# A third of the modulation as two-row products, the rest beside the projections, and residual adds on VectorE

## Chip, core, metric

The kernel runs on one core of a Trainium2 chip. The metric is the device time of one execution, in microseconds (us). A launch runs two transformer blocks after one another; the change touches the first.

## What is computed

The first block (sequence 1024, model width 1024, context 256) is, cut to what matters here:

```python
sh1, sc1, gt1, sh2, sc2, gt2 = split(silu(c) @ w_ada + b_ada, 6)        # w_ada: 1024 x 6144
csh1, csc1, ...              = split(silu(c_ctx) @ w_ada + b_ada, 6)    # only csh1, csc1 are used
hc = rmsnorm(ctx, g_pre_mix) * (1 + csc1) + csh1                        # then its k, v, gates
hx = rmsnorm(x, g_pre_mix) * (1 + sc1) + sh1                            # then @ w_in, token mixers
x  = x + gt1 * rmsnorm(yx @ w_out, g_post_mix)
hx = rmsnorm(x, g_pre_ffn) * (1 + sc2) + sh2
x  = x + gt2 * rmsnorm(conv_ffn(hx), g_post_ffn)
```

All is float32. The modulation is a product of two vectors (`silu(c)`, `silu(c_ctx)`) with a 24 MB matrix. Its rows sh1 and sc1 (with csh1, csc1) are wanted at once; gt1, sh2, sc2 and gt2 only after the token mixers.

## The kernel before

The block is a row of stages (`with Stage(...)`). Between two stages all engines meet at a barrier, so a stage begins when the last engine has left the one before. Each engine runs its own list in order; semaphores join them.

`stage_modulation` ("mod"). SP loads `w_ada` in 12 pieces of 2 MB (512 columns each) into four buffers `ada_w`; row 8p+k of the matrix is on partition p, in slot k. VectorE forms, per piece, the sum over k = 0..6 of `silu(c)[8p+k] * w[8p+k, :]` (lines 341 and 345), for the first four pieces for both condition vectors, so 16 chains of 7. ScalarE makes the eighth product (296). TensorE then sums over the partitions with a 128 x 128 matrix of ones, so that every partition holds the row, and adds the bias with a third matmul on one partition (373 to 375, `over_partitions`). ScalarE copies the rows out (302, 323). At the end VectorE multiplies five rows with the gains `graw` (359, 362) and the stage waits for `x` and `ctx`.

`stage_norm_turn` ("norm1") normalises 8 + 2 tiles with these rows and transposes them.

`stage_project_mix` ("mix") multiplies them with `w_in`. Products are split in high and low parts of type F32R: ScalarE makes the high part of the weights (208), VectorE the low one (213), TensorE runs three matmuls (219 to 221). First come 40 steps of 256 KB of weights (`w_tm`, SP line 594, two buffers; a load waits until the low part of two steps before is made, ScalarE waits until TensorE has used the step two before). A step is 12 matmuls of 512 columns, in its third group (steps 16 to 23) 6. Then come 17 blocks of 512 KB (`w_cm`, 601): 5 with a copy out by VectorE (706), then 12 with the short convolution on VectorE.

`stage_gla` works through the chunks; VectorE updates the state (950), then copies the next chunk's q and k (966, 967), on which TensorE waits (1018).

`stage_into_stream` is used as "mix_out" (8 blocks of weights, two groups of 4 token tiles) and "ffn_down" (22 blocks, two groups): split, multiply, and after each group, per tile: ScalarE sums the squares (1221), VectorE scales and roots with ScalarE (1252, 1212, 1255) and writes `y = product * inverse * gate row` (1259); GpSimd adds `y` to `x` (1234). `y` is one buffer, so the next tile's line 1259 waits for GpSimd. TensorE's next group waits tile by tile for line 1259 (`taken`), and VectorE's next split stands behind all four tiles. A third user of this function, in the second block, has no gate row; nothing of its order changes.

Of the kernel before, what the change touches and what calls it, by code (L numbers as in the profile page):

```python
# [17 lines left out]
ALU = mybir.AluOpType  # L18
ACT = mybir.ActivationFunctionType
AX = mybir.AxisListType.X  # L20
P = 128
# [3 lines left out]
D = 1024  # L25
# [202 lines left out]
def stage_modulation(core):  # L228

# [8 lines left out]
    csil = core.at("cond_silu", 108.25, [P, 2, KD])  # L238
    ones = core.at("ones", 109, [P, P])
    scaled = [core.at(f"scaled_rows{n}", kb, [P, 512]) for n, kb in enumerate((110, 202))]  # L240
    bias = core.at("ada_bias", 178, [1, 6 * D])
    SUMMED = KD - 1
    graw = core.at("gain_rows", 150, [P, 4, D])
# [3 lines left out]
    with Stage(core, "mod") as s:  # L247
        (masks_in, x_in, ctx_in, cond_in, param_in, bias_in, gain_in, silu_done, zeroed, params_turned,
         params_out, rows_done, ctx_rows_done, combined, order, sum_mm, ctx_sum, ctx_mm) = s.sems(
            "masks_in", "x_in", "ctx_in", "cond_in", "param_in", "bias_in", "gain_in", "silu_done",  # L250
            "zeroed", "params_turned", "params_out", "rows_done", "ctx_rows_done", "combined", "order",
            "sum_mm", "ctx_sum", "ctx_mm")
        scaled_done = s.sem("scaled_done")
        w_in = [s.sem(f"w_in{j}") for j in range(NW)]
        summed = [s.sem(f"summed{j}") for j in range(NW)]
        n_par = sum(len(t) for t in PARAM_ROWS)

        @s.b.gpsimd
        def _(pool):
            nc.gpsimd.memset(ones[:], 1.0).then_inc(zeroed, 1)  # L260

        @s.b.sync
        def _(sp):
# [4 lines left out]
            sp.dma_start(bias[:], dram["b_ada"]).then_inc(bias_in, 16)  # L268

            def load(i, before):  # L270
                for j in range(NW):
                    if before is not None:

                        sp.wait_ge(sum_mm, before * NW + (j + 1))
                    sp.dma_start(ada_w[:, j], dram["w_ada"][0].rearrange("(p k) n -> p k n", k=KD)
                                 [:, :, bass.ds(i * (512 * NW) + 512 * j, 512)]).then_inc(w_in[j], 16)
            run_loop(sp, 3, load)

        @s.b.scalar
        def _(act):  # L280
            act.wait_ge(cond_in, 32)
            nc.scalar.activation(csil[:], cvec[:], ACT.Silu).then_inc(silu_done, 1)
            act.dma_start(core.masks.ap().rearrange("p a b -> p (a b)"), dram["masks"]).then_inc(masks_in, 16)
# [6 lines left out]
            act.dma_start(core.ctx[:], dram["ctx"][0].rearrange("(t p) d -> p t d", p=P)).then_inc(ctx_in, 16)  # L290
            act.dma_start(core.x0[:], dram["x"][0].rearrange("(t p) d -> p t d", p=P)).then_inc(x_in, 16)
            for g, name in enumerate(("g_pre_mix", "g_post_mix", "g_pre_ffn", "g_post_ffn")):
                act.dma_start(graw[:, g, :], dram[name].to_broadcast([P, D])).then_inc(gain_in, 16)

            def scale(j, v, n):
                nc.scalar.activation(scaled[n][:], ada_w[:, j, SUMMED], ACT.Copy,
                                     scale=csil[:, v, SUMMED:SUMMED + 1]).then_inc(scaled_done, 1)

            def take(i, j):

                act.wait_ge(sum_mm, i * NW + j)
                nc.scalar.activation(flat_rows[:, bass.ds(i * (512 * NW) + 512 * (j - 1), 512)],
                                     ps[:, (j - 1) % NW, :], ACT.Copy).then_inc(rows_done, 1)

            def evacuate(i, before):
                for j in range(NW):
                    act.wait_ge(w_in[j], i * 16 + 16)
                    if before is None:
                        if j == 0:
                            act.wait_ge(silu_done, 1)  # L310
                        else:

                            act.wait_ge(sum_mm, j)
                        scale(j, 1, 0)
                        scale(j, 0, 1)
                    else:
                        act.wait_ge(sum_mm, i * NW + (j - 1 if j else 0))
                        scale(j, 0, j % 2)
                    if before is not None or j:
                        take(i, j)  # L320
                    if before is None:
                        act.wait_ge(ctx_mm, j + 1)
                        nc.scalar.activation(flat_rows[:, 6 * D + 512 * j:6 * D + 512 * j + 512],
                                             ps[:, 4 + (j + 1) % 4, :], ACT.Copy).then_inc(ctx_rows_done, 1)
            run_loop(act, 3, evacuate)
            take(3, 0)

# [2733 lines left out]
```

## Time and profile before

| | us |
|---|---|
| median of 3 runs (3810.71 to 3820.34) | 3814.72 |
| the profiled execution, its own time | 3825.96 |
| its span in the trace | 3824.1 |
| mod, up to norm1's first instruction | 120.8 |
| norm1 | 44.0 |
| mix, the 40 steps | 107.9 |
| mix_out with its entry and exit | 125.9 |

A view of the trace is one execution. "Granted clock" is the mean TensorE clock of a stretch: 1.00 is 2.4 GHz, 0.50 is 1.2 GHz. A row of the timeline merges neighbours of one kind (x2, x8) and shows in brackets how long the engine sat idle before and what ended that.

### The profile page before, as it was taken

Reading aid. Unit: us, or ns where it says so; the run is one execution under the profiler, and the core shown is the slowest. Engines: PE = TensorE matmul, PEld = TensorE weight load, DVE = VectorE, ACT = ScalarE, POOL = GpSimd, SP = SyncE. Lnnn points to the kernel's source line nnn. Section 1 sums busy time; section 2 is a strip of 40 time slices with the busy share of each in tenths; the row PEclk is TensorE's granted clock in tenths of the full one; section 3 lists DMA queues with packets and bytes.
Section 4 is the critical chain, followed back from the end, with each engine's and each line's share of the span. In section 5 each row is a group of like instructions: output and inputs, shape, how many; then the busy total and the mean of one; then the engine's idle time right before and its main releaser. Section 6 shows DMA issues by size and latency. Waiting matters only on the chain. (4 is left out here: it accounts for less than half of the span.)

```text
span 3824.1 us, 58374 instructions
## 1 busy us (share of the span) xinstructions
PE 3169.6 (83%) x24565; PEld 2477.3 (65%) x24565; DVE 2125.8 (56%) x2592; ACT 1340.5 (35%) x1776; POOL 381.6 (10%) x249
## 2 busy tenths in 40 slices
PE   6699956679999899587987878858799872999995
PEld 1378845568888678473666574747566662888884
DVE  6632254356666533427366665767211347988885
ACT  1320143322111232327333333434200222777774
POOL 0200011210000000302011111111000000122120
PEclk7699967879999999799998888969899976999997
DMA  8131102211111323200201010010310334999996
GB/s 323 57 101 40 38 1 95 82 44 50 49 44 51 108 88 102 79 18 28 68 2 66 1 43 24 4 47 18 102 50 22 127 139 154 377 395 396 399 394 214
DMA packets 219997, 424.22 MB, mean 111 GB/s; under 512 B 13120, under 2 KB 122642, under 8 KB 219538
## 3 DMA queue, kind: packets, MB, share of 16 engines
q1 hardware_dynamic: 212434, 394.75, 29.0%
q0 software_dynamic: 4608, 16.78, 1.7%
q10 hardware_dynamic: 2753, 9.66, 0.6%
q8 instruction: 167, 2.74, 0.3%
q14 instruction: 35, 0.29, 0.0%
HBM read 387.61 MB, written 33.55 MB: 110 GB/s over the span
## 5 line engine op out<-in xcount | busy, mean ns | idle before, releaser
L213 DVE TENSOR_TENSOR w_exp_low<-w_exp,w_exp_high 128x2048 fp32r<-128x2048 f32 x192 | 437.7, 2290 | 54.2 <-ACT w_exp_high L208 54.2
L208 ACT ACTIVATE w_exp_high<-w_exp 128x2048 fp32r<-128x2048 f32 x192 | 368.0, 1920 | 123.2 <-PE psum L221 123.2
L219 PE MATMUL psum<-ffn_high,w_high 128*128 128x512 f32 x704 | 275.0, 391 | 9.2 <-DVE w_low L213 9.2
L220 PE MATMUL psum<-ffn_low,w_high 128*128 128x512 f32 x704 | 274.8, 390 | 0.0
L221 PE MATMUL psum<-ffn_high,w_low 128*128 128x512 f32 x704 | 274.8, 390 | 0.0
L1375 DVE SCALAR_TENSOR_TENSOR ffn_hidden<-u_padded,param_columns,ffn_hidden 128x1024 f32 (+1 forms) x176 | 226.2, 1285 | 23.8 <-DVE ffn_hidden L1371 0.2
L219 PE MATMUL psum<-w_exp_high,x_turned_high 128*128 128x512 f32 x512 | 202.9, 396 | 7.0 <-DVE w_exp_low L213 7.0
L221 PE MATMUL psum<-w_exp_high,x_turned_low 128*128 128x512 f32 x512 | 200.0, 391 | 0.0
L220 PE MATMUL psum<-w_exp_low,x_turned_high 128*128 128x512 f32 x512 | 199.8, 390 | 0.0
L2301 DVE COPY inverse<-psum 64x512 f32<-64x512 f32 x192 | 121.8, 637 | 75.5 <-PE psum L2136 50.4
L219 PE MATMUL psum<-ffn_down_w_split,ffn_down_lhs_split 128*128 128x512 f32 x352 | 140.6, 400 | 23.3 <-DVE ffn_down_lhs_split L213 17.4
L219 PEld LDWEIGHTS psum<-ffn_high,w_high 128*128 128x128 f32 x704 | 132.8, 189 | 37.3 <-DVE w_low L213 9.6
L2235 ACT ACTIVATE inverse<-psum 64x512 f32<-64x512 f32 x192 | 107.0, 557 | 130.3 <-PE psum L2136 105.2
L220 PEld LDWEIGHTS psum<-ffn_low,w_high 128*128 128x128 f32 x704 | 132.7, 189 | 27.7
L221 PEld LDWEIGHTS psum<-ffn_high,w_low 128*128 128x128 f32 x704 | 132.7, 189 | 27.6
L2573 DVE TENSOR_TENSOR gates_sb<-gates_sb,psum 128x1024 f32<-128x1024 f32 x16 | 19.5, 1221 | 232.3 <-PE psum L2521 232.3
L513 PE MATMUL psum<-masks,norm_h 128*128 128x128 f32 x272 | 60.4, 397 | 102.1 <-POOL norm_h L502 63.9
L213 DVE TENSOR_TENSOR ffn_down_w_split<-ffn_down_ring,ffn_down_w_split 128x1024 fp32r<-128x1024 f32 x44 | 53.9, 1225 | 158.7 <-ACT ffn_down_lhs_split L208 158.7
L220 PE MATMUL psum<-ffn_down_w_split,ffn_down_lhs_split 128*128 128x512 f32 x352 | 139.6, 397 | 0.0
L221 PE MATMUL psum<-ffn_down_w_split,ffn_down_lhs_split 128*128 128x512 f32 x352 | 139.3, 396 | 0.0
L1350 ACT ACTIVATE ffn_hidden<-ffn_hidden (+1 forms) x22 | 23.3, 1061 | 295.4 <-DVE ffn_hidden L1375 295.4
L219 PE MATMUL psum<-mix_out_w_split,mix_out_lhs_split 128*128 128x512 f32 x256 | 102.8, 402 | 27.7 <-DVE mix_out_lhs_split L213 20.9
(431 smaller groups left out, 7867.4 us busy)
## 6 DMA issues: line engine op xcount, KB each, us to landing
w_exp<-in_exp_w_gate SPq DMA_DIRECT2D x32, 2048.0 KB, 11.1
w_exp<-in_exp_w_up SPq DMA_DIRECT2D x32, 2048.0 KB, 10.4
w_exp<-in_exp_w_down SPq DMA_DIRECT2D x32, 2048.0 KB, 11.2
ada_weights<-in_w_ada SPq DMA_DIRECT2D x12, 2048.0 KB, 14.0
w_raw<-in_w_up SPq DMA_DIRECT2D x44, 512.0 KB, 3.8
ffn_down_ring<-in_w_down SPq DMA_DIRECT2D x44, 512.0 KB, 3.6
mix_out_ring<-in_w_out SPq DMA_DIRECT2D x32, 512.0 KB, 3.7
mixers_hT<-hidden SPq DMA_DIRECT2D x4, 4096.0 KB, 13.0
```

Of the source, the lines that this page charges most:

```text
L208: return nc.scalar.activation(out, src, ACT.Copy, scale=scale)
L213: return nc.vector.tensor_tensor(out, src, high.bitcast(F32), ALU.subtract)
L219: nc.tensor.matmul(out, left[0], right[0], start=start, stop=False)
L220: nc.tensor.matmul(out, left[0], right[1], start=False, stop=False)
L221: return nc.tensor.matmul(out, left[1], right[0], start=False, stop=stop)
L513: ins = nc.tensor.transpose(ps[:, 2 * (t % 4) + k // 4, (k % 4) * P:(k % 4 + 1) * P], hbuf[:, t % SLOTS, k * P:(k + 1) * P], core.mask(M_ID))
L1350: nc.scalar.activation(block(i * 2 + (j - 1)), block(i * 2 + (j - 1)), ACT.Silu).then_inc(silu_done, 1)
L1375: ins = nc.vector.scalar_tensor_tensor(out=out, in0=src, scalar=weight, in1=out, op0=ALU.mult, op1=ALU.add)
L2235: nc.scalar.activation(place[rows[1], :], ps[rows[1], inverse_bank(n, 1), columns], ACT.Copy).then_inc(inv_lower[n % 2], 1)
L2301: nc.vector.tensor_copy(place[rows[0], :], ps[rows[0], inverse_bank(n, 0), columns]).then_inc(inv_upper[n % 2], 1)
L2573: nc.vector.tensor_tensor(sg[:, h], sg[:, h], ps[:, 4 * h + 2:4 * h + 4, :], ALU.mult).then_inc(parts, 1)
```

## The change

- Mod computes only the first 4 of the 12 pieces. TensorE multiplies them directly: the stationary operand is `csil[:, k, :]`, 128 rows by 2 columns (both conditions), the moving one a slot of `ada_w`; 8 matmuls of 512 columns per piece give a pair of rows in PSUM. VectorE adds the bias (`pairs`, 2 x 512). A second matmul per row, with a 2 x 128 selector, spreads it to all partitions; ScalarE copies the shifts out, VectorE the gain rows with `(1 + scale) * g`. `x` and `ctx` are loaded by SP behind the four pieces.
- The other 8 pieces (rows of `c` alone) move into mix: SP loads them in 16 halves of 1 MB into two buffers, VectorE adds slot after slot into `mod_rows`, 64 instructions put by the list `room` behind its work of each step, and TensorE sums over the partitions with one matmul of ones after each of blocks 5 to 12; ScalarE copies out. The bias goes into partition 0 by DMA after GpSimd has zeroed the rows.
- The three later gain rows are loaded and multiplied in gla, by VectorE, before its loop.
- In `stage_into_stream` the add moves from GpSimd to VectorE, with four `y` buffers: in the middle of a product one add behind each of the next splits, at the end interleaved.

```diff
@@ stage_modulation, TensorE
+            def spread_rows(j):
+                pe.wait_ge(pair_done, j + 1)
+                if j >= 2:
+                    pe.wait_ge(shifts_done, 2 * j - 2)
+                for v in range(2):
+                    nc.tensor.matmul(ps[:, spread_bank(j, v), :], select[:, v, :], pairs[:, j], start=True, stop=True
+                                     ).then_inc(spread, 1)
+            pe.wait_ge(silu_done, 1)
+            pe.wait_ge(selects, 2)
+            for j in range(NW):
+                pe.wait_ge(w_in[j], 16)
+                for k in range(KD):
+                    ins = nc.tensor.matmul(ps[0:2, j, :], csil[:, k, :], ada_w[:, j, k], start=(k == 0),
+                                           stop=(k == KD - 1))
+                ins.then_inc(pair_mm, 1)
+                if j:
+                    spread_rows(j - 1)
...
+            spread_rows(NW - 1)
@@ stage_project_mix
+    room = [0] * 5 + [2] * 3 + [1] * 5 + [2] * 3 + [0] * (KD + 2) + [1] * 3 + [2] * (3 + KD) + [4] * (irregular + 1)
+    step_of = [at for at, n in enumerate(room) for _ in range(n)][:4 * HALVES]
+    last_step = [step_of[4 * h + 3] for h in range(HALVES)]
+    ada_loads = {0: [0, 1]}
+    for h in range(2, HALVES):
+        ada_loads.setdefault(last_step[h - 2] + (3 if last_step[h - 2] + 3 < NQ else 4), []).append(h)
@@ TensorE
+                if n in sums_at:
+                    m = n - irregular
+                    first = ADA + 512 * m
+                    pe.wait_ge(ada_used, 2 * m + 2)
+                    if m >= 2:
+                        pe.wait_ge(ada_out, m - 1)
+                    nc.tensor.matmul(ps[:, 6 + m % 2, :], core.ones[:], flat_rows[:, first:first + 512], start=True,
+                                     stop=True).then_inc(ada_sum, 1)
@@ VectorE
+            def modulate(step):
+                for m in [m for m, at in enumerate(step_of) if at == step]:
...
+                    if k == 0:
+                        dve.wait_ge(ada_in[h % 2], 16 * (h // 2 + 1))
...
+                    ins = nc.vector.scalar_tensor_tensor(out=acc, in0=ada_w[:, h % 2, k], scalar=core.csil[:, n, 0:1],
+                                                         in1=acc, op0=ALU.mult, op1=ALU.add).then_inc(ada_order, 1)
@@ stage_gla, VectorE
+            dve.wait_ge(gain_in, 48)
+            nc.vector.tensor_tensor(rows[:, R_GP1], rows[:, R_GP1], graw[:, 0], ALU.mult)
+            nc.vector.scalar_tensor_tensor(out=rows[:, R_G2], in0=rows[:, R_G2], scalar=1.0, in1=graw[:, 1],
+                                           op0=ALU.add, op1=ALU.mult)
+            nc.vector.tensor_tensor(rows[:, R_GP2], rows[:, R_GP2], graw[:, 2], ALU.mult)
@@ stage_into_stream
-        if gate_row is not None:
-            @s.b.gpsimd
-            def _(pool):
-                pool.wait_ge(x_in, 16)
-                for t in range(TT):
-                    pool.wait_ge(taken, t + 1)
-                    nc.gpsimd.tensor_tensor(x[:, t], x[:, t], y[:], ALU.add).then_inc(added, 1)
+            def add(t):
+                dve.wait_ge(x_in, 16)
+                dve.wait_ge(taken, t + 1)
+                nc.vector.tensor_tensor(x[:, t], x[:, t], y[t % G][:], ALU.add).then_inc(added, 1)
```

VectorE's list in mix, around the step in which the fifth half (the second use of buffer 0 after its reload) begins; the change alone. `mix_tm_high` is the high part of a step's weights, `mix_ada_in0` the landing of a half in buffer 0, `mix_ada_order` the instruction before:

```order
L213 TENSOR_TENSOR w_tm_split<-w_tm,w_tm_split 128x512 [waits mix_tm_high]
L690 SCALAR_TENSOR_TENSOR mod_rows<-ada_weights_late,cond_silu,mod_rows 128x512 [waits mix_ada_order] x2
L213 TENSOR_TENSOR w_tm_split<-w_tm,w_tm_split 128x512 [waits mix_tm_high]
L690 SCALAR_TENSOR_TENSOR mod_rows<-ada_weights_late,cond_silu,mod_rows 128x512 [waits mix_ada_order]
L690 SCALAR_TENSOR_TENSOR mod_rows<-ada_weights_late,cond_silu,mod_rows 128x512 [waits mix_ada_order,mix_ada_in0]
L213 TENSOR_TENSOR w_tm_split<-w_tm,w_tm_split 128x512 [waits mix_tm_high] x2
```

Before, the same place held only the rows of line 213. The low part of step 16 now stands behind an instruction that waits for the load of half 4, which SP issues with step 16's own weights.

VectorE's list in mix_out where the second group begins; the change alone (waits left out, since semaphores are numbered anew there). The numbers behind `mix_out_y` are the four buffers:

```order
L1289 SCALAR_TENSOR_TENSOR mix_out_y_3800<-psum,mix_out_stat,mod_rows 128x1024
L213 TENSOR_TENSOR mix_out_w_split<-mix_out_ring,mix_out_w_split 128x1024
L213 TENSOR_TENSOR mix_out_lhs_split<-gla_out_cm,mix_out_lhs_split 128x512
L1267 TENSOR_TENSOR x_stream<-x_stream,mix_out_y_3797 128x1024
L213 TENSOR_TENSOR mix_out_w_split<-mix_out_ring,mix_out_w_split 128x1024
L213 TENSOR_TENSOR mix_out_lhs_split<-gla_out_cm,mix_out_lhs_split 128x512
L1267 TENSOR_TENSOR x_stream<-x_stream,mix_out_y_3798 128x1024
```

Before, the list was the same without line 1267, which GpSimd ran in its own list.

## Rows read from the trace of the kernel before

**Rows 1.** The page, its part 1: busy time of TensorE and GpSimd.

```profile
PE 3169.6 (83%) x24565; PEld 2477.3 (65%) x24565; DVE 2125.8 (56%) x2592; ACT 1340.5 (35%) x1776; POOL 381.6 (10%) x249
```

**Rows 2.** Windows: mod, mix's 40 steps, its later blocks, mix_out; then DMA's rate.

```profile
core 0: us, PE busy (x) PEld busy (x) DVE busy (x) ACT busy (x) POOL busy (x), PEclk, DMA share, GB/s
0.00:120.80 120.80, 74.84 (x99) 22.74 (x99) 85.51 (x120) 21.14 (x34) 0.41 (x5) 0.74 0.76 280
164.80:272.70 107.90, 100.16 (x425) 80.63 (x426) 33.62 (x50) 28.51 (x45) 0.00 (x0) 0.96 0.36 99
345.00:480.00 135.00, 130.84 (x576) 108.03 (x576) 35.95 (x31) 15.55 (x15) 1.76 (x4) 0.99 0.16 40
15.00:30.00 15.00, 5.44 (x9) 2.07 (x10) 10.06 (x15) 1.93 (x3) 0.00 (x0) 1.00 1.03 402
```

**Rows 3.** Mod: VectorE's group of line 345, its wait for the weights, norm1's first instruction.

```profile
L345 DVE SCALAR_TENSOR_TENSOR mod_rows<-ada_weights,cond_silu,mod_rows 128x512 f32<-128x512 f32 (+1 forms) x96 | 72.2, 752 | 3.4
DVE mod_rows L341 <- DMA ada_weights<-in_w_ada: 27.5, 7, 15.8
120.83 1.28 ACT L431 ACT_TABLE_LOAD   x1 [6.59 <-PEq L185]
```

**Rows 4.** DMA issues: KB each, median us from issue to landing.

```profile
ada_weights<-in_w_ada SPq DMA_DIRECT2D x12, 2048.0 KB, 14.0
w_tm<-in_w_in SPq DMA_DIRECT2D x40, 256.0 KB, 2.6
alibi<-in_alibi SPq DMA_DIRECT2D x1, 1536.0 KB, 6.0
```

**Rows 5.** Timeline: weight loads of float32 matmuls of 512 columns in a row.

```profile
483.90 0.33 PEld L780 LDWEIGHTS psum<-gate_low,w_gates 32*128 32x128 f32 x1 [0.52 <-issue]
484.76 0.33 PEld L780 LDWEIGHTS psum<-gate_low,w_gates 32*128 32x128 f32 x1 [0.52 <-issue]
```

**Rows 6.** Windows (columns as in rows 2): stretches with TensorE busy, and what followed.

```profile
41.00:44.40 3.40, 3.40 (x4) 0.99 (x4) 0.00 (x0) 0.52 (x1) 0.00 (x0) 0.50 1.04 399
44.40:47.80 3.40, 1.25 (x3) 0.29 (x2) 3.23 (x5) 1.81 (x3) 0.00 (x0) 0.99 1.05 386
170.90:174.20 3.30, 3.30 (x9) 2.53 (x9) 0.00 (x0) 0.00 (x0) 0.00 (x0) 0.50 0.42 148
174.20:177.60 3.40, 3.40 (x17) 2.78 (x16) 0.69 (x1) 0.63 (x1) 0.00 (x0) 1.00 0.09 11
481.20:494.30 13.10, 13.10 (x18) 5.79 (x18) 6.01 (x4) 7.84 (x7) 0.00 (x0) 0.50 0.00 0
```

**Rows 7.** Timeline of mix: VectorE at step 16, ScalarE at step 18.

```profile
213.64 0.69 DVE L213 TENSOR_TENSOR w_tm_split<-w_tm,w_tm_split 128x512 fp32r<-128x512 f32 x1 [2.03 <-ACT w_tm_split L208]
217.07 0.63 ACT L208 ACTIVATE w_tm_split<-w_tm 128x512 fp32r<-128x512 f32 x1 [0.74 <-DMA w_tm<-in_w_in]
```

**Rows 8.** Timeline: gain products at mod's end; gla's first wait of TensorE for VectorE.

```profile
114.58 3.48 DVE L359 SCALAR_TENSOR_TENSOR mod_rows<-mod_rows,gain_rows 128x1024 f32<-128x1024 f32 x3
117.98 2.35 DVE L362 TENSOR_TENSOR mod_rows<-mod_rows,gain_rows 128x1024 f32<-128x1024 f32 x2
532.55 2.08 PE L1018 MATMUL psum<-q_chunk,k_chunk 64*128 64x128 f32 x16 [2.04 <-DVE k_chunk L967]
```

**Rows 9.** Timeline of mix_out (first six rows) and ffn_down (last): scales and adds.

```profile
684.70 1.28 DVE L1259 SCALAR_TENSOR_TENSOR mix_out_y<-psum,mix_out_stat,mod_rows 128x1024 f32<-128x1024 f32 x1
686.31 0.17 DVE L1255 RECIPROCAL mix_out_stat<-mix_out_stat 128x1 f32<-128x1 f32 x1 [0.27 <-ACT mix_out_stat L1212]
688.63 1.28 DVE L1259 SCALAR_TENSOR_TENSOR mix_out_y<-psum,mix_out_stat,mod_rows 128x1024 f32<-128x1024 f32 x1 [2.15 <-POOL x_stream L1234]
698.66 2.86 DVE L213 TENSOR_TENSOR mix_out_lhs_split<-gla_out_cm,mix_out_lhs_split 128x512 fp32r<-128x512 f32 x1
738.70 1.28 DVE L1259 SCALAR_TENSOR_TENSOR mix_out_y<-psum,mix_out_stat,mod_rows 128x1024 f32<-128x1024 f32 x1
751.48 2.34 POOL L1234 TENSOR_TENSOR x_stream<-x_stream,mix_out_y 128x1024 f32<-128x1024 f32 x1 [1.47 <-DVE mix_out_y L1259]
1434.04 2.86 DVE L213 TENSOR_TENSOR ffn_down_lhs_split<-ffn_hidden,ffn_down_lhs_split 128x512 fp32r<-128x512 f32 x1
```

More of the change, by code:

```diff
@@ L299, in take @@
[L299 to L324, printed above, removed]
@@ L348, in _, with gains @@
-            run_loop(dve, 3, sums)
+            dve.wait_ge(masks_in, 16)
+            for v in range(2):
+                nc.vector.tensor_copy(select[:, v, :], core.masks[0:2, M_ID, v:v + 1].to_broadcast([2, P])
+                                      ).then_inc(selects, 1)
+            dve.wait_ge(bias_in, 16)
+            def gains(j):
+                for v in range(2):
+                    dve.wait_ge(spread, 2 * j + v + 1)
+                    first = 512 * (j - 2)
+                    nc.vector.scalar_tensor_tensor(out=place(j, v), in0=ps[:, spread_bank(j, v), :], scalar=1.0,
+                                                   in1=graw[:, first:first + 512], op0=ALU.add, op1=ALU.mult
+                                                   ).then_inc(gains_done, 1)
@@ L350, in _ @@
+            for j in range(NW):
+                dve.wait_ge(pair_mm, j + 1)
+                nc.vector.tensor_tensor(pairs[:, j], ps[0:2, j, :], bias[:, 512 * j:512 * j + 512], ALU.add
+                                        ).then_inc(pair_done, 1)
+            dve.wait_ge(gain_in, 16)
+            gains(2)
+            gains(3)
             dve.wait_ge(params_turned, 1)
@@ L553, in stage_project_mix @@
     scx = core.at("sc_part", 40, [P, T])
+    flat_rows = core.rows.ap().rearrange("p a d -> p (a d)")
+    ada_w = core.at("ada_weights_late", 170, [P, 2, KD // 2, 512])
+    ADA, HALVES = 2 * D, 2 * (4 * D // 512)
     def tokens(k, t0, n):
@@ L1242, in split, with out @@
                 low_part(nc, l_split[:, q % 2, 1], lhs(k, g), l_split[:, q % 2, 0]).then_inc(low, 1)
-            def out(g):
+            def add(t):
+                dve.wait_ge(x_in, 16)
+                dve.wait_ge(taken, t + 1)
+                nc.vector.tensor_tensor(x[:, t], x[:, t], y[t % G][:], ALU.add).then_inc(added, 1)
+            def out(g, k):
+                if k:
+                    if gate_row is not None:
+                        add(g * G + k - 1)
+                    return
                 for t in range(g * G, g * G + G):
@@ L1256, in out @@
                     dve.wait_ge(order, 2 * t + 2)
-                    if t:
-                        dve.wait_ge(added, t)
-                    nc.vector.scalar_tensor_tensor(out=y[:], in0=product(t), scalar=stat[:, 0, t:t + 1], in1=gate_row,
-                                                   op0=ALU.mult, op1=ALU.mult).then_inc(taken, 1)
+                    if t >= G:
+                        dve.wait_ge(added, t - G + 1)
+                    nc.vector.scalar_tensor_tensor(out=y[t % G][:], in0=product(t), scalar=stat[:, 0, t:t + 1],
+                                                   in1=gate_row, op0=ALU.mult, op1=ALU.mult).then_inc(taken, 1)
+                    if k is None and t > g * G:
+                        add(t - 1)
+                if k is None and gate_row is not None:
+                    add(g * G + G - 1)
             with_splits(split, out)
```

182 lines of the change are left out of this document (89 added, 93 removed).

## The prediction

> **What bounds the kernel now.** I read the page first: TensorE is busy 83% of the span, GpSimd 10% [rows 1]. Then the windows of the stages that the change touches. In mod TensorE is busy 74.84 of 120.80 us, VectorE 85.51, DMA moves 280 GB/s [rows 2]: no engine is full, and a chain bounds the stage. Its longest member is VectorE's sums: line 345 alone takes 72.2 us, 96 times 752 ns, and VectorE waits 27.5 us more for weights, 15.8 of them for the first piece [rows 3]. Mod ends when norm1's table load starts, at 120.83. In mix TensorE bounds: busy 100.16 of 107.90 us in the 40 steps (VectorE 33.62) and 130.84 of 135.00 in the later blocks [rows 2]. VectorE has room there, TensorE has none, so whatever goes on TensorE in mix is paid in full. In mix_out and ffn_down the waits around the end of a group are the place: the scale of a tile waits 2.15 us for GpSimd's add of the one before [rows 9].
>
> **Mod.** Removed: all 16 chains and their matmuls. New is a chain of SP, TensorE and a short end.
>
> The first piece. Before, it was there at 15.8 us, beside masks, parameters and a part of `ctx` on the other queue. Now masks, one gain row and parameters stand beside it, and `x` and `ctx` come later: I take 14.0, with 12 and 15.8 as ends. Further pieces of 2 MB at 402 GB/s [rows 2] come every 5.2 us, and all the rest (6.3 MB of weights, 5.2 MB of `x` and `ctx`) is in by 14.0 + 11.5/0.402 = 43 us.
>
> TensorE. A float32 matmul call leaves two records. At 1.2 GHz, records of 512 columns start 0.86 us apart (483.90, 484.76) [rows 5]; at 2.4 GHz half of it, 0.43. The products are 4 pieces x 8 slots x 2 = 64 records, the spreads 8 x 2 = 16. At 1.2 GHz a piece takes 13.7 us, at 2.4 GHz 6.9: either is more than the 5.2 us of a load, so from the first piece on TensorE is the bound and does not stop. Which clock is the large question. The nearest rows: float32 matmuls of 128 rows by 512 columns kept the engine busy from 41.0 to 44.4 at a granted 0.50, and it was 0.99 after that; the F32R matmuls of mix did the same at 174.2, 4.5 us after their start. Against it: line 780, with 32 of 128 rows [rows 5], was busy 13.10 of 13.10 us and stayed at 0.50 [rows 6]. The new products fill all 128 rows but 2 of 128 columns, and no row here shows that shape. I take the rise, because the data streamed through the engine, 128 rows of 512 float32, is that of the first of these rows. With 5.1 us at 1.2 GHz (6 records), 58 x 0.43 = 24.9 us for the other products, 16 x 0.43 = 6.9 for spreads, some 2 us for changes between the two shapes and 0.5 for the transposes, TensorE ends at 14.0 + 5.1 + 24.9 + 6.9 + 2.5 = 53.4. VectorE's last gain row (0.75, like line 345) and parameter copies (0.6) lie behind it, less what overlaps; barrier 0.5. Norm1 starts at 54.8 instead of 120.8: **-66.0**. `x` at 43 is hidden, with 10 us to spare.
>
> **Mix, the 40 steps.** The 64 accumulations of 0.75 us lie beside TensorE. A step is 2.72 us; VectorE has 0.61 (low part), at times 0.6 (copy out), and at most 2 x 0.78: 2.2 of 2.72. Cost nothing while TensorE has 12 matmuls a step; if that cover is gone (steps 16 to 23, half as long), `room` has zeros. The loads are another matter. 1 MB: between 2.6 us for 256 KB and 6.0 for 1536 KB [rows 4] I estimate 4.7, with the step's weights in front 5.4. In steps 31 to 39 a half is issued 5.4 us before its use and TensorE's own slack is 1.4 more: nothing. The half used at step 15 is the exception (the first order listing): it is issued with step 16's weights, 3.5 us before VectorE arrives, so VectorE waits 2 us; the low part of step 16, at 213.64 before [rows 7], slips by 1.5, and steps 16 to 23 are paced by loads (ScalarE waits for DMA at 217.07 [rows 7]) that are issued behind low parts, so it is not caught up: +1.5. The weights behind each 1 MB land up to 0.7 us later, in a slack of 1.3 before ScalarE; for step 19 perhaps 0.5. **+2.0**, with 0 and 8 as ends (8 if the halves of steps 31 to 39 each stall 1 us more). GpSimd's zeroing of 4096 elements and SP's wait for it end before step 2's load is due.
>
> **Mix, the blocks.** TensorE is full there [rows 2], so 8 sums of ones cost 8 x 2 x 0.43 = **+6.9**; with a start-up each up to 9. ScalarE's 8 copies and VectorE's waits for the last halves (each half is issued behind the low part of a block of 10.9 to 13.8 us) are hidden; a half later than 6.5 us would hold the copy of the next block: 0 to 2.
>
> **Gla.** Three gain products, at 1.16 each as in mod [rows 8], stand between the second state update and the q and k copies on which TensorE waits (532.55, idle 2.04) [rows 8]: **+3.5**. The three loads of 512 KB are issued 9 us earlier, hidden; ends 0 and 5.
>
> **Mix_out and ffn_down.** In the middle, scales came 3.85 us apart: 684.70, 688.63, and so on to 696.33. Without the wait a tile takes what leads from one scale to the next reciprocal, 684.70 to 686.31, and 0.2: 1.81. Three tiles save 6.1. The split behind them took 2.86 instead of 0.68 while GpSimd added [rows 9]: another 2.2. The next product starts 8.2 us earlier, the same in ffn_down, where the split at 1434.04 shows the same 2.86 [rows 9]: -16.6 with its slightly longer first wait. The adds (1.16 each) follow a split of 1.8 within a step of 5.4: hidden. At the end of each: scales from 738.70, then per tile scale 1.2, add 1.15, statistics and root 0.6; the last add ends at 749.9 instead of 751.48 + 2.34 = 753.8 [rows 9]. Less 0.4 for stores closer together: -3.5 each. **-23.6** in all; ends -28 and -14.
>
> **Sum.** -66.0 + 2.0 + 6.9 + 3.5 - 23.6 = **-77.2**. Against the profiled execution's own 3825.96 that is 3748.8; that execution stands 11.2 us above the median of the runs, so for the median 3814.72 - 77.2 = **3737.5**.
>
> **Rivals.**
> (B) The clock stays at 1.2 GHz in mod. For it speaks line 780 [rows 6]; against it the stretches of 128 rows. Then 80 records x 0.86 + 3 = 71.8 us follow 14.0, mod ends at 87.2 with its tail, and 32 of the 66 are gone: 3814.7 - 45 = **3770**. [...]
> (C) Slower than before: the loads in mix hold VectorE, and with it the low parts. It decides from the point where 1 MB takes over 7.2 us (5.4 and the slack of 1.8). The row for it is mod's own 14.0 [rows 4], of twice the size and beside another queue: 13 halves x 6.8 = 88, and 9 times a step's high and low part laid bare, 12: 3737 + 100 = **3837**. Against it: 256 KB in 2.6 us and DMA at 99 GB/s in these steps [rows 2]; the new loads bring it to some 200 of 402.
> (D) The moved adds return what they save: if each of the first three adds held a split, 2 x 3 x 1.2, and the end gained nothing: 3737 + 14 = **3752**; inside the range.
> (E) Mod waits for `x` instead of TensorE. It would have to land after 54, so all loads run below 290 GB/s from 14.0 on, against the 402 [rows 2] of before; at mod's own mean of 280 [rows 2] it costs 1 us and leaves the sum as it is.
>
> **Chances.** My forecast with its variants (D, E) 0.70, B 0.25, C 0.02; 0.03 for something that returns nearly all. A change under 0.3% (11.4 us) can't be told from none here. Faster 0.96, same 0.02, slower 0.02. The likeliest case's own range is 3728 to 3748; the range given has to reach B: 3728 to 3774.
>
> **What would show it.** In the profile after: norm1's table load near 55 (B: near 87); the granted clock over mod's products 1.00 after the first 3 to 7 us (B: 0.50), and product records 0.43 apart; a wait of VectorE for `ada_weights_late` of about 2 us once and none over 1 us in steps 31 to 39 (C: many of 5 and more); TensorE's line 628 with 16 records of 0.6; in gla TensorE's first wait for `k_chunk` 5.5 instead of 2.04; four scales 1.8 apart. Wrong in the main thing if mod ends where B says.

## The result, and the profile after

| us | before | changed |
|---|---|---|
| median of the runs | 3814.69 (3810.71 to 3820.34, 4 runs) | 3746.51 (3742.48 to 3755.25, 4 runs) |
| ratio | | 0.9823, 95% interval 0.9801 to 0.9845 |
| the same pair in a later comparison | 3823.80 (9 runs) | 3752.93 (5 runs), ratio 0.9819, 0.9803 to 0.9834 |
| profiled execution, its span | 3825.96, 3824.1 | 3742.48, 3740.7 |

The forecast was 3737.5 in a range of 3728 to 3774; 68 to 71 us came where 77 were expected. Between the two profiled executions it is 83.5 us, where the forecast had 3748.8 for the second and 3742.48 came. The time by stage tells more. Each stage starts with a table load of ScalarE (ACT_TABLE_LOAD, 1.28 us), and the difference of two of them is a stage's length. Two profiles of each kernel stand side by side; the second ones are runs 9 and 12 below.

| stage, us | before | before, 2nd | changed | changed, 2nd | forecast of the change |
|---|---|---|---|---|---|
| mod | 120.83 | 117.46 | 54.80 | 54.79 | -66.0 |
| norm1, gla_out, norm2 | 107.1 | 107.1 | 107.4 | 107.4 | 0 |
| mix | 312.70 | 310.00 | 325.01 | 324.56 | +8.9 |
| gates and gla | 127.59 | 127.83 | 130.48 | 130.69 | +3.5 |
| mix_out | 125.64 | 127.14 | 112.68 | 113.08 | -11.8 |
| ffn_up | 497.23 | 497.64 | 496.11 | 496.29 | 0 |
| ffn_down | 279.03 | 279.20 | 264.51 | 264.52 | -11.8 |
| up to norm3 | 1570.1 | 1566.3 | 1491.0 | 1491.3 | |
| the second block, whose code is the same | 2254.0 | 2255.6 | 2249.7 | 2261.9 | 0 |

**Mod.** The page's part 1, which answers to [rows 1]:

```profile
PE 3129.3 (84%) x24565; PEld 2456.4 (66%) x24565; DVE 2108.9 (56%) x2568; ACT 1327.3 (35%) x1756; POOL 344.6 (9%) x234
```

Windows of mod (columns as in [rows 2]):

```profile
0.00:54.80 54.80, 38.36 (x83) 8.40 (x83) 6.34 (x13) 3.89 (x7) 0.41 (x5) 0.99 0.76 282
...
14.00:19.90 5.90, 4.98 (x6) 0.76 (x7) 0.00 (x0) 0.00 (x0) 0.00 (x0) 1.00 1.02 365
19.90:31.20 11.30, 11.30 (x27) 2.13 (x25) 0.68 (x1) 0.00 (x0) 0.00 (x0) 1.00 1.05 393
```

And the timeline of TensorE there, with norm1's first instruction, which stood at 120.83 in [rows 3]:

```profile
14.92 16.38 PE L338 MATMUL psum<-ada_weights,cond_silu 128*2 128x512 f32 x32 [14.92 <-DMA ada_weights<-in_w_ada]
31.23 1.98 PE L331 MATMUL psum<-row_pairs,select_row 2*128 2x512 f32 x4
33.14 7.03 PE L338 MATMUL psum<-ada_weights,cond_silu 128*2 128x512 f32 x16
...
51.30 1.98 PE L331 MATMUL psum<-row_pairs,select_row 2*128 2x512 f32 x4
...
54.80 1.28 ACT L381 ACT_TABLE_LOAD   x1 [12.08 <-PEq L185]
```

VectorE's 85.5 us are gone and TensorE works without a stop from the first piece on. The sum's units are in the traces: a float32 matmul call left two records (line 338: 64 for 32 calls; line 780 of before: 24 for 12), and records of 512 columns started 0.86 us apart at a granted 0.50 [rows 5, 6] and 0.43 apart at 1.00 (19.90:31.20 above). The profile prints the granted clock only as a share; 1.2 and 2.4 GHz are the forecast's names for 0.50 and 1.00, and nothing is worked out from them. Six records took the first 5 us (0.81 to 0.86 us apart), the other 26 of the first 32 are 0.43 apart (the second window counts the sixth once more): the clock rose as forecast, after 6 records. The window prints a clock of 1.00 for both stretches, but the trace's first entry of the clock stands at 19.96 us; before it the spacing of records is the better witness.

**Mix.** Its waits of VectorE and TensorE (line waited for, total, times, longest), and three rows of its timeline:

```profile
DVE mod_rows L690 <- DMA ada_weights_late<-in_w_ada: 28.4, 9, 6.3
PE psum L219 <- DVE w_tm_split L213: 13.6, 6, 6.9
PE psum L219 <- ACT out_gate L638: 3.2, 1, 3.2
PE psum L219 <- DVE qT L721: 2.2, 1, 2.2
```

```profile
110.94 0.63 ACT L208 ACTIVATE w_tm_split<-w_tm 128x512 fp32r<-128x512 f32 x1 [7.97 <-DMA w_tm<-in_w_in]
...
144.43 0.45 SPq L562 DMA_DIRECT2D ada_weights_late<-in_w_ada  x1
...
151.26 0.75 DVE L690 SCALAR_TENSOR_TENSOR mod_rows<-ada_weights_late,cond_silu,mod_rows 128x512 f32<-128x512 f32 x1 [3.85 <-DMA ada_weights_late<-in_w_ada]
```

The places can be read off the low parts (VectorE L213), 57 in both kernels, each counted from its own mix's start. The low part of step 2 is 2.08 us later than before and that of steps 4 to 15 is 1.15; step 16 is 4.30 later, steps 19 to 39 some 5.2. (Seven profiles have this mix: here, runs 1, 3, 5, 6, 7 and 9. Step 39 is 4.1 to 5.5 later in them.) In the blocks each sum of ones then adds 0.905:

```profile
308.23 1.22 DVE L213 TENSOR_TENSOR w_cm_split<-w_cm,w_cm_split 128x1024 fp32r<-128x1024 f32 x1 [9.11 <-ACT w_cm_split L208]
...
320.01 1.23 DVE L213 TENSOR_TENSOR w_cm_split<-w_cm,w_cm_split 128x1024 fp32r<-128x1024 f32 x1 [5.97 <-ACT w_cm_split L208]
```

The group of the sums on TensorE (busy, mean ns of one, idle before):

```profile
L628 PE MATMUL psum<-mod_rows,ones 128*128 128x512 f32 x16 | 8.2, 590 | 0.0
```

It is 11.78 us from one block's low part to the next, 10.88 before; eight sums are 7.2. Between, after step 41, TensorE waits 3.2 us for `out_gate` in every profile (3.5 in run 11). In the first profile of before the granted clock was at 0.50 for 6.8 us around the end of that wait, in its second not at all, in the changed kernel for 3.4: so mix of before was 312.7 and 310.0, and the changed one is 12.3 or 15.0 longer, by which profile of before one takes. Run 2, whose mix is that of before, has 312.8.

**Gla** lost what was forecast. TensorE's first wait for `k_chunk` was 2.04 in [rows 8]:

```profile
478.16 1.23 DVE L1006 TENSOR_TENSOR mod_rows<-mod_rows,gain_rows_late 128x1024 f32<-128x1024 f32 x1
479.31 1.21 DVE L1007 SCALAR_TENSOR_TENSOR mod_rows<-mod_rows,gain_rows_late 128x1024 f32<-128x1024 f32 x1
480.44 1.21 DVE L1009 TENSOR_TENSOR mod_rows<-mod_rows,gain_rows_late 128x1024 f32<-128x1024 f32 x1
...
482.52 2.08 PE L1046 MATMUL psum<-q_chunk,k_chunk 64*128 64x128 f32 x16 [5.45 <-DVE k_chunk L990]
```

**Mix_out and ffn_down.** The scales of mix_out, the split and the first add, then the end, which answer to [rows 9]:

```profile
633.20 1.28 DVE L1289 SCALAR_TENSOR_TENSOR mix_out_y<-psum,mix_out_stat,mod_rows 128x1024 f32<-128x1024 f32 x1
...
635.01 1.28 DVE L1289 SCALAR_TENSOR_TENSOR mix_out_y<-psum,mix_out_stat,mod_rows 128x1024 f32<-128x1024 f32 x1
...
641.05 0.68 DVE L213 TENSOR_TENSOR mix_out_lhs_split<-gla_out_cm,mix_out_lhs_split 128x512 fp32r<-128x512 f32 x1
641.65 1.22 DVE L1267 TENSOR_TENSOR x_stream<-x_stream,mix_out_y 128x1024 f32<-128x1024 f32 x1
...
678.92 1.28 DVE L1289 SCALAR_TENSOR_TENSOR mix_out_y<-psum,mix_out_stat,mod_rows 128x1024 f32<-128x1024 f32 x1
...
687.82 2.35 DVE L1267 TENSOR_TENSOR x_stream<-x_stream,mix_out_y 128x1024 f32<-128x1024 f32 x2
```

The scales are 1.81 apart, as forecast. From the first scale to the split's end it is 8.5 us instead of 16.8 (684.70 to 701.52), from the first scale of the end to the end of the last add 11.25 instead of 15.1. From the first scale of the middle to the first scale of the end ffn_down gained 10.3 us where mix_out gained 8.3, for another reason: the clock. The same 3.6 us behind the split, before and then changed:

```profile
1437.00:1440.60 3.60, 3.60 (x9) 2.83 (x10) 1.83 (x2) 0.65 (x2) 0.00 (x0) 0.51 0.67 156
```

```profile
1363.20:1366.80 3.60, 3.60 (x16) 2.96 (x17) 3.12 (x4) 1.53 (x2) 0.00 (x0) 1.00 0.46 146
```

Nine products instead of sixteen. Before, TensorE waited 6.9 us in all for these scales and the split (longest 2.6), its products stood 0.43 apart instead of 0.23 from 1429.20 on, and the granted clock was still 0.50 to 0.51 here; in the changed kernel none of these waits is over 0.2 us and the clock is 1.00. At half the speed these 3.6 us cost 1.8.

### The profile page after: what moved, and what is told of

The parts are those of the page before. It is cut to its first block and busy times, and to the rows that moved or that the text cites. A ratio compares the mean times of both kernels' runs of the same rounds, so it can differ in the third digit from the quotient of the medians.

```text
span 3740.7 us, 58197 instructions
## 1 busy us (share of the span) xinstructions
PE 3129.3 (84%) x24565; PEld 2456.4 (66%) x24565; DVE 2108.9 (56%) x2568; ACT 1327.3 (35%) x1756; POOL 344.6 (9%) x234
## 5 line engine op out<-in xcount | busy, mean ns | idle before, releaser
L213 DVE TENSOR_TENSOR w_exp_low<-w_exp,w_exp_high 128x2048 fp32r<-128x2048 f32 x192 | 437.7, 2290 | 54.2 <-ACT w_exp_high L208 54.2
L221 PEld LDWEIGHTS psum<-ffn_high,w_low 128*128 128x128 f32 x704 | 132.6, 188 | 27.5
L213 DVE TENSOR_TENSOR ffn_down_w_split<-ffn_down_ring,ffn_down_w_split 128x1024 fp32r<-128x1024 f32 x44 | 53.9, 1225 | 152.0 <-ACT ffn_down_lhs_split L208 152.0
L1909 PE MATMUL psum<-mixers_hT,w_rkv 128*128 128x512 f32 x288 | 124.9, 593 | 0.0
```

The lines of the kernel that those rows point to most:

```text
L213: return nc.vector.tensor_tensor(out, src, high.bitcast(F32), ALU.subtract)
L221: return nc.tensor.matmul(out, left[1], right[0], start=False, stop=stop)
L1909: ins = nc.tensor.matmul(ps[:, 2 * NEXT[n] + h, :], w[n][:, kt], hT[:, kt, 512 * h:512 * h + 512], start=(kt == 0), stop=(kt == KD - 1))
```

## Experiments

The untouched second block took 2250 to 2266 us over all profiles. The touched stages repeat more closely. Where their code is the changed kernel's, ffn_down took 263.5 to 264.6 us, mix_out 112.5 to 113.7, mod 53.35 to 55.16 (its first piece came at 13.9 to 15.4) and mix 324.2 to 325.1, in two profiles 327.0 and 327.3 (see run 8). Where it is that of before, mod took 117.5 to 121.3 and mix 310.0 to 312.8. So sizes below are read from stages, each good to about such a spread, and the medians only where they tell kernels apart. Times of before run on the same chip stand with each group.

### Runs 1 to 3: the residual adds

Beside a before of 3818.50 (3809.93 to 3825.03). Run 1 puts `stage_into_stream` back as it was:

```diff
+    y = core.at(f"{name}_y", scratch_kb + 4, [P, D])
...
+            @s.b.gpsimd
...
+                    nc.gpsimd.tensor_tensor(x[:, t], x[:, t], y[:], ALU.add).then_inc(added, 1)
...
-                      (132, 136, 140, 144))
```

> The changed kernel with stage_into_stream as it was before: one buffer y, the add on GpSimd. The theory of the prediction (mix_out and ffn_down give 23.6 us, and in the two profiles they gave 13.0 + 14.5 = 27.5): this run takes 24 to 28 us more than the changed kernel, 3770 to 3775, 41 to 45 below the kernel before. Rival: the untouched stages drifted by some 5 us between the two profiles, and a part of the 27.5 is such drift; then it lies 15 to 20 us above the changed kernel.

Measured: 3777.41 (3774.20 to 3778.80), ratio 0.9890 against 0.9823 and 0.9819 of the changed kernel: 26 us above it. Mix_out 126.7, ffn_down 278.0: +14.0 and +13.5. The theory holds; what differed between profiles lies elsewhere.

Run 2 is the kernel before with only the new `stage_into_stream`.

> The kernel before with only the new stage_into_stream. If the parts of the change are independent, 24 to 28 us below the kernel before (3787 to 3791), with mix_out some 12 to 13 and ffn_down some 12 to 14.5 shorter in the profile and everything else unchanged. Rival: the parts share something (another start of the transfers, another clock), and this one and the one with the stream undone do not add up to the whole, by more than 5 us.

Measured: 3792.97 (3786.99 to 3803.88), ratio 0.9931 (0.9918 to 0.9945), 25.5 us below before. Mix_out 113.7, ffn_down 264.3: -12.0 and -14.8. Run 1 lies 41.1 below before and this one 25.5: 66.6 together, against 68 to 71 for the whole, within the 5 us that the rival asked for. The parts are independent as far as that tells.

Run 3 keeps the four buffers and gives the adds back to GpSimd:

```diff
-                nc.vector.tensor_tensor(x[:, t], x[:, t], y[t % G][:], ALU.add).then_inc(added, 1)
...
+                    nc.gpsimd.tensor_tensor(x[:, t], x[:, t], y[t % G][:], ALU.add).then_inc(added, 1)
```

> The changed kernel with four buffers y but the adds on GpSimd, as before. It tells the buffer from the engine. By the prediction's split of the middle (6.1 us from the wait, 2.2 from the stretched split behind it): the scales come 1.8 apart, but GpSimd still adds (2.35 each, four in a row behind the scales), VectorE's splits beside it are stretched to some 2.9, once or more often, and at the end of each stage the last add ends some 4 us after the last scale: 3 to 10 us slower than the changed kernel, 3749 to 3757. Rival: the buffer is everything and the engine nothing: the same as the changed kernel within 2 us. Second rival: GpSimd slows every VectorE operation beside it, the scales too, and half of the gain is lost (12 us or more).

Measured: 3763.24 (3760.96 to 3767.07), ratio 0.9853. Mix_out 118.2, ffn_down 270.0: each 5.5 above the changed kernel and 8.0 to 8.5 below run 1. Of the 27.5 us the buffers give 16.5 and the engine 11.0, which is more than my 3 to 10. The size is near the second rival's 12, its mechanism did not come: the scales still take 1.28 and stand 1.81 apart. Timeline behind the first group of mix_out, and TensorE's clock after it:

```profile
634.53 10.39 POOL L1262 TENSOR_TENSOR x_stream<-x_stream,mix_out_y 128x1024 f32<-128x1024 f32 x4 [64.39 <-DVE mix_out_y L1290]
...
638.54 1.28 DVE L1290 SCALAR_TENSOR_TENSOR mix_out_y<-psum,mix_out_stat,mod_rows 128x1024 f32<-128x1024 f32 x1
639.81 2.92 DVE L213 TENSOR_TENSOR mix_out_w_split<-mix_out_ring,mix_out_w_split 128x1024 fp32r<-128x1024 f32 x1
...
642.65 2.82 DVE L213 TENSOR_TENSOR mix_out_lhs_split<-gla_out_cm,mix_out_lhs_split 128x512 fp32r<-128x512 f32 x1
...
645.52 0.80 PE L219 MATMUL psum<-mix_out_w_split,mix_out_lhs_split 128*128 128x512 f32 x1 [3.98 <-DVE mix_out_lhs_split L213]
```

```profile
645.60:651.60 6.00, 6.00 (x14) 4.71 (x15) 1.61 (x2) 0.00 (x0) 0.00 (x0) 0.50 0.62 178
```

Both splits beside the queued adds are stretched (2.92 and 2.82 instead of 1.22 and 0.68: +3.8 us), and TensorE, which waited 4.0 us for them, runs its next 6 us at a granted 0.50 (14 products where 26 would go: some 2.7 us). Less 0.8 that this kernel gains at the end and 0.4 at its start, that is about the 5.5. At the end the buffers alone do the work: from the first scale of the end to the next stage it is 18.2 us before, 14.5 in the changed kernel and 13.7 here, so there the move to VectorE costs 0.8. The scale beside the same adds keeps its 1.28. The splits read both inputs from SBUF, the scale one of them from PSUM; whether this is the cause, no run shows.

### Run 4: where the late loads stand in mix

```diff
-    room = [0] * 5 + [2] * 3 + [1] * 5 + [2] * 3 + [0] * (KD + 2) + [1] * 3 + [2] * (3 + KD) + [4] * (irregular + 1)
+    room = [0] * 5 + [2] * 3 + [1] * 5 + [2] * 2 + [1] + [0] * (KD + 3) + [2] * (5 + KD) + [4] * (irregular + 1)
...
-    ada_loads = {0: [0, 1]}
+    ada_loads = {2: [0], 3: [1], KD * 3: [4], KD * 3 + 1: [5]}
...
```

> The changed kernel with the late modulation halves loaded elsewhere: halves 0 and 1 behind the weights of steps 2 and 3 and not in front of step 2's, half 4 and 5 with steps 24 and 25 and not with 16 and 18, and no sum of half 4 in step 15. In the profiles mix's 40 steps lost 1.15 us at step 2 (its weights behind 2 MB) and 4.0 at steps 15 to 19. Theory: both come from the place of these loads in SP's queue, and go: low part of step 39 is 0 to 0.5 us later than before instead of 5.2, the kernel 4 to 5.5 us faster than the changed one. Rival: the loss at steps 16 to 19 is DMA shared among all (short steps paced by loads that only got slower) and comes back wherever the 1 MB lands: then 1 to 2 us at most.

Measured in the profile: mix 321.3 instead of 325.0 (324.2 to 325.1 in the five profiles without the fall of the clock of run 8). The low part of step 2 is 0.5 us earlier than before, that of step 23 0.6 earlier; then steps 24 to 28, where halves 4 and 5 now land, lose 1.6, and step 39 is 1.0 later than before, where the changed kernel is 5.2 later. So 4.2 of the 5.2 us (3.0 to 4.5, against each of the seven profiles) hung on the place of these loads in SP's queue, and the rival has the rest: 1 MB landing between short loads cost something at the new place too. The median, 3751.12 (3747.32 to 3754.68), ratio 0.9822 (0.9809 to 0.9835), can't be told from the changed kernel's: 4 us drown in the second block, which took 2265.6 us in this profile, the longest of all.

### Runs 5 and 6: TensorE's clock in mod

Each with a single execution, beside a before of 3821.86. Run 5 takes 32 of the 128 rows, and so leaves out three quarters of each sum:

```diff
-                    ins = nc.tensor.matmul(ps[0:2, j, :], csil[:, k, :], ada_w[:, j, k], start=(k == 0),
+                    ins = nc.tensor.matmul(ps[0:2, j, :], csil[0:32, k, :], ada_w[0:32, j, k], start=(k == 0),
```

> The changed kernel with the products of mod over 32 of the 128 rows of each slot (so the modulation sums a quarter of its terms); 2 output columns as before, and all loads unchanged. Record spacing in mod: 0.85 us at 1.2 GHz, 0.43 at 2.4. My reason for the high clock was the 128 rows of data streamed through the engine, as against line 780 of before with 32 rows: then the products stay 0.85 apart throughout and mod ends near 87 us instead of 54.8. Rival: the rows do not decide, an engine that is kept busy without a gap rises either way: then mod ends at 54.8 as in the changed kernel, and line 780 stayed low for another reason.

```profile
15.35 27.46 PE L338 MATMUL psum<-ada_weights,cond_silu 32*2 32x512 f32 x32 [15.35 <-DMA ada_weights<-in_w_ada]
...
46.45 13.81 PE L338 MATMUL psum<-ada_weights,cond_silu 32*2 32x512 f32 x16
```

32 records in 27.46 us, 16 in 13.81: 0.86 each, from the first to the last, without a gap in 66 us. The spreads, which are the same in both kernels, stand 0.85 to 1.0 us apart here and 0.43 to 0.54 in the changed kernel, so it is the clock and not the shape of the product; the trace's first entry of the clock is only at 140.3 us. Mod ends at 87.3, rival B's 87.2. With the same loads and as many products the clock rose after 5 us for 128 rows and not for 32, as in line 780 [rows 6]: the ground on which the forecast chose between its two prices is shown.

Run 6 issues piece j only behind piece j-1's products, so that TensorE waits:

```diff
+                if j:
+                    sp.wait_ge(pair_mm, j)
                 sp.dma_start(ada_w[:, j], dram["w_ada"][0].rearrange("(p k) n -> p k n", k=KD)
```

> The changed kernel with each piece of 2 MB in mod issued only when the products of the piece before are done, so that TensorE waits some 7 us (2 MB at 390 to 400 GB/s and the start) before each of the pieces 1 to 3. [...] Worst case: 4 pieces x 13.7 + 3 x 7 + 15 + 4 = 95 us for mod. Theory that a wait of this length costs the clock for as long as the first start did (6 records): each piece 6.9 + 2.5 = 9.4, mod ends near 15 + 4 x 9.4 + 3 x 7 + 4 = 78. Rival, the clock survives a wait of 7 us: mod ends near 54.8 + 21 - 6 = 70.

```profile
14.56 9.52 PE L340 MATMUL psum<-ada_weights,cond_silu 128*2 128x512 f32 x16 [14.56 <-DMA ada_weights<-in_w_ada]
32.73 8.97 PE L340 MATMUL psum<-ada_weights,cond_silu 128*2 128x512 f32 x16 [8.65 <-DMA ada_weights<-in_w_ada]
...
50.24 8.75 PE L340 MATMUL psum<-ada_weights,cond_silu 128*2 128x512 f32 x16 [6.63 <-DMA ada_weights<-in_w_ada]
...
68.44 9.89 PE L340 MATMUL psum<-ada_weights,cond_silu 128*2 128x512 f32 x16 [7.54 <-DMA ada_weights<-in_w_ada]
```

After each wait (6.6 to 8.7 us) the first 4 to 7 records are 0.85 apart, at a granted 0.50, and the rest 0.43, at 0.99 to 1.00: a piece takes 8.8 to 9.9 us instead of 7.03. The worst case, every record 0.85 apart, did not come, and the clock did not survive the wait either. Mod ends at 85.45, more than my 78, because 8.5 to 9.5 us passed from one piece's end to the next start instead of 7, and 7.1 us from the last piece's end to norm1 instead of 4 (the last spreads were 0.85 apart again). In the changed kernel, whose pieces are queued at once, TensorE's only wait for a piece is the first, of 14.92 us, and its products are 0.43 apart from the seventh record on.

### Runs 7 and 8: an earlier start, and sums where TensorE waits

Also one execution each. Run 7 loads every piece as two halves with a wait each:

```diff
+                for a in range(2):
+                    sp.dma_start(ada_w[:, j, 4 * a:4 * a + 4], dram["w_ada"][0].rearrange("(p k) n -> p k n", k=KD)
+                                 [:, 4 * a:4 * a + 4, 512 * j:512 * j + 512]).then_inc(w_in[2 * j + a], 16)
```

> The changed kernel with each 2 MB piece of mod loaded as two transfers of 1 MB (slots 0 to 3, 4 to 7), each with its own wait. TensorE is the bound of mod from the first piece on (72 of its records in one stretch), so an earlier start should move the whole stage: first product near 10 instead of 14.92, mod ends 4 to 5.5 us earlier (49 to 51 instead of 54.8). Rival: the stage is then bound by the loads (x and ctx in at 43, weights at 29) or the two halves land together, and less than 2 us come of it.

First product at 9.79, mod 50.13 instead of 54.80: -4.7 (-3.2 to -5.0 against the six profiles with whole pieces). TensorE was the bound of the whole stage, and `x`, which the sum called hidden with 10 us to spare, still was.

Run 8 moves the sums of ones and the gain products:

```diff
 stage_gates, tensor, behind u == 3
+            for m in range(8):
+                nc.tensor.matmul(ps[:, late_bank[m], :], core.ones[:], late(m), start=True, stop=True
+                                 ).then_inc(ada_sum, 1)
...
 stage_gla, vector, first step, behind qk_staged
+                        nc.vector.tensor_tensor(rows[:, R_GP1], rows[:, R_GP1], graw[:, 0], ALU.mult)
...
```

> The changed kernel with the eight sums of ones moved out of mix's blocks, where TensorE is full, to the end of TensorE's work in gates, where it waits 23 us for gla (ScalarE copies them out in its own waits of 2.0 and 6.1 us there), and the three gain products of gla moved from in front of the q and k copies into VectorE's waits within the first step. Theory: mix gets 7.2 us shorter (8 x 0.905; 325.0 to 317.8), gates and gla together 3.4 us (130.5 to 127.1), 10 to 11 in all. Rival: ScalarE's copies in gates push its exponentials (its waits there are for VectorE, so a copy that comes late holds the chain): gates gets 1 to 4 us longer and half of it is given back.

Measured: mix 319.7 (-5.3), gates and gla 127.7 (-2.8). The eight steps of 11.78 are 10.88 again, so the 7.2 are there. But 1.9 came back, 1.6 of it at one place, TensorE's wait for the `qT` copy at the start of block 5: there VectorE was held by the late halves (four waits of 5.4 to 6.5 us there), the wait is 1.4 us in before, 2.2 in the changed kernel and 2.5 here, and behind it the clock fell in this run:

```profile
284.40:287.80 3.40, 3.40 (x9) 2.64 (x8) 0.96 (x2) 0.00 (x0) 0.00 (x0) 0.50 0.81 222
```

That fall does not belong to this edit. It stands at the same place in runs 5 and 6, whose mix is the changed kernel's and took 327.3 and 327.0 us, and in none of the other five profiles of that mix. Nor does the length of the wait decide alone: the fall came behind waits of 2.3 and 3.5 us there and not behind one of 2.6 in run 1. The rival on ScalarE in gates did not come.

### Runs 9 to 11: the changed kernel again, and all mended

Beside a before of 3823.80 (3813.02 to 3827.49). Run 9 is the changed kernel; run 10 the edits of runs 4, 7 and 8 together.

> The changed kernel itself, unchanged, beside the next two on the same chip. The untouched stages (the second block) varied by 10 us between the profiles so far, the touched ones by 0.3, so the stage sums (-66.0, +12.3, +2.9, -13.0, -14.5: -78 us) should come again within 1 us, while the median lies 66 to 82 us under that of the kernel before. Rival: the median difference of the first comparison, 68.2 us, is the true one, because the new kernel loses some 10 us in untouched stages each time: then their sum in this profile is again above that of before.

> The changed kernel with the three mendings that were measured apart: half pieces in mod (-4.7), late loads moved in mix (-4.2 in the 40 steps), sums of ones in gates and gain products in gla's waits (mix -7.2 without the clock's dip, gates and gla -2.8). Additive: 18 to 20 us below the changed kernel of this call in the touched stages, about 3728 if that is 3747. Rival: a part is given back by the clock (each new wait of TensorE in mix's blocks of 2.6 us or more can start a stretch of 3.4 us at 1.2 GHz, 1.7 us each): 14 to 17.

Run 9: 3752.93 (3750.09 to 3759.27), the stages within 0.5 us of the first profile (table). Run 10: 3733.62 (3724.95 to 3735.57), ratio 0.9759 (0.9742 to 0.9776), 19.3 us below run 9 and 90 below before. Mod 49.50 (-5.3), mix 314.8 (-9.8), gates and gla 127.8 (-2.9): 18.0 in stages. The rival is in it too: the fall of the clock at block 5 came in this run as in run 8 (and as in runs 5 and 6, without these edits).

Run 11 adds a warm-up before the first piece:

```diff
+            pe.wait_ge(ones_done, 1)
+            for n in range(24):
+                nc.tensor.matmul(ps[:, 3, 0:P], ones[:], ones[:], start=True, stop=True)
```

> The kernel of e10 with 24 products of 128 x 128 ones (discarded) on TensorE from 1 us on, before the first piece of mod is there at 9.8. If what the clock needs is a busy engine, it is high when the first products start: all records 0.43 apart, mod 2.6 us shorter (6 records x 0.43). Rival: the small products (128 columns) do not raise it, or the engine is still in them when the piece lands: mod the same or up to 2 us longer.

```profile
1.00 8.51 PE L336 MATMUL psum<-ones 128*128 128x128 f32 x48 [1.00 <-POOL ones L263]
9.44 3.60 PE L343 MATMUL psum<-ada_weights,cond_silu 128*2 128x512 f32 x8
14.19 3.60 PE L343 MATMUL psum<-ada_weights,cond_silu 128*2 128x512 f32 x8 [1.16 <-DMA ada_weights<-in_w_ada]
```

The discarded products go from 0.21 to 0.11 apart after 6 us, and the real ones are 0.43 apart from the first. But of the 2.6 us at most a part arrives: mod is 48.77, 0.7 less than in run 10 and 1.4 less than in run 7, whose mod is the same as run 10's. The engine now waits 1.16 us for the second half, at 14.19, and 0.46 for the next piece, at 18.25. The bound has moved to the loads. 3732.23 (3728.25 to 3738.63), the same as run 10.

### Run 12: the kernel before again

> The kernel before, unchanged, for a second profile of it. Open is why the medians differ by 68 to 71 us where the touched stages differ by 79: if the time behind norm3's start is taken as median less 1.8 less the end of ffn_down in the profile, it is 2243 to 2252 us for the kernel before and 2254 to 2263 for all with the new mod. First reading: the first profile of before (3825.96) was a slow one and its untouched part is normally some 8 us shorter: then this profile is near 3815, with norm3 starting at 1570.1 within 0.5 and the rest 2243 to 2250. Second reading: the rest is 2254 here too, with the same span near 3824, and profiles of this kernel are slower than its other executions. Third: norm3 starts earlier than 1570, so that the stages of the first block vary in this kernel.

Measured: 3820.54 (3813.42 to 3823.81, 11 runs), span 3821.9, norm3 at 1566.3, the rest 2255.6. The third reading holds in part: mod was 3.4 us shorter (VectorE waited 24.4 us for weights, 27.5 in [rows 3]) and mix 2.7 (no fall of the clock after step 41), while mix_out was 1.5 longer for a fall of its own. Run 2, whose mod and mix are those of before, has 121.3 and 312.8, as the first profile. So the first block gained some 75 to 79 us by the profiles and 68 to 71 by the medians. The remaining 4 to 11 us lie in the second block, whose code is the same and which varied by 16 us between profiles. It took 2254.0 to 2256.8 us in the three profiles with the old mod and 2249.7 to 2265.6, 2259.4 in the mean, in the eleven with the new one. Whether it is a little longer behind the new first block, or this is chance, stays open.

## Why the prediction was right

**Mod: right, in size and reason.** The sum gave norm1 at 54.8; it was 54.80. The first piece came at 14.92 instead of 14.0 and TensorE ended a little earlier than 53.4 in return. The choice of the full clock rested on the 128 rows against line 780's 32, and run 5 shows that difference. Against the second profile of before, whose own loads were faster, the same end is worth 62.7 instead of 66.0; against run 2's mod it is 66.5.

**Mix, the 40 steps: the mechanism right, the size off.** The sum had +2.0 (ends 0 and 8), measured 5.2 (4.1 to 5.5). Two steps of it failed. "GpSimd's zeroing and SP's wait for it end before step 2's load is due" was true of the issue (4.2 us after mix's start, 4.8 before) and missed the transfer: step 2's weights stood behind 2 MB and landed 7.9 us after their issue, not 2.6 (+1.15). At step 15 the wait of "2 us" was 3.85, since 1 MB behind the step's weights took 6.8 us and not 5.4; and the next 256 KB loads, behind this 1 MB and the one issued at 153.01, came late in the very steps that are paced by loads, where nothing catches up: 4.0 instead of 1.5. In steps 31 to 39 it held but for the sign: one wait reached 1.25 us (1.88 in run 9) where none over 1 was expected, and none cost time. The load on the DMA was as forecast, 199 GB/s over the steps for "some 200".

**Mix, the blocks.** Sums 7.2 for 6.9 (0.905 each, where two records are 0.86). "0 to 2" for late halves was 0.8, at the `qT` copy, and 2.5 and 3.7 in the two profiles where the clock fell behind it. By the first profile of before mix lost 12.3, by the second 15.0; 2.4 of these 2.7 us are the clock after step 41.

**Gla: right.** +2.9 for 3.5; the wait was 5.45 for 5.5.

**Mix_out and ffn_down: right, a little small.** Middle 8.3 for 8.2, end 3.7 for 3.5 each, in ffn_down some 2 more from the clock, which the sum did not look for, and 1.5 at the two stages' starts: -27.5 for -23.6. The end was right in size, but run 3 shows that the four buffers bring it and the move to VectorE does not.

**The sum** for the first block was 77.2, and 75 to 79 came: mix's error and the streams' nearly cancel, so the total is better than its parts, and that much is luck. The median, 9.0 us above the forecast, is still inside the likeliest case's own 3728 to 3748, but only by 1.5; by the profiles the missing part lies in the second block, where the forecast expected no change; why stays open. Of the rivals, B came with 32 rows (run 5) and not in this kernel, C did not come (nine waits of VectorE for halves, 28.4 us, all but 6.0 of it in the blocks, where it has room), D and E neither.

## What to carry to other kernels

A large load that hides in an engine's slack can still be seen by the small loads queued behind it (256 KB behind 2 MB landed 7.9 us after their issue, not 2.6): cost the place in the queue, not only the time to its own use, and above all in front of steps that the small loads pace. Work for a full engine can be free one stage later, where that engine waits (run 8: mix -5.3, gates and gla -2.8); run 10 got 18 us by moving and halving alone. And a wait taken off TensorE's path is worth more than its length where the clock would have fallen behind it (the middle of ffn_down gained 10.3 us, that of mix_out 8.3).

## What the runs showed that was not expected

- Records of products of 128 rows by 2 columns went from 0.86 to 0.43 us apart after 5 us; those of the same products over 32 rows stayed 0.86 apart for 66 us without a gap (run 5).
- Waits of TensorE of 2 to 4 us cost a stretch of 3.4 or 6.8 us at a granted 0.50 in some executions and none in others, at the same place in the program: the 3.2 us wait in mix came with 6.8, 0 and 3.4 us of it (both profiles of before, the changed kernel), the `qT` wait of 2.0 to 3.5 us with 3.4 us in two of the seven profiles of the changed mix.
- GpSimd's adds stretched VectorE's splits (0.68 to 2.8, 1.22 to 2.9) and not its scales (1.28), which read PSUM (run 3).
- The untouched second block varies by 16 us between profiles (2249.7 to 2265.6), four times what moving the loads in mix brings: a gain of 4 us is seen in its stage and not in the median.
